# Two-block transformer on one core: the first scale taken as rows turned to columns, the first shift on VectorE, eight projection groups between them

## What is computed

```python
cond = jax.nn.silu(c)
mod = cond @ w_ada + b_ada                         # 2048 -> 6 * 2048
sh1, sc1, gt1, sh2, sc2, gt2 = jnp.split(mod, 6)
h = rms_norm(x, g_pre_mix) * (1.0 + sc1) + sh1
p = h @ w_in + b_in                                # 2048 -> 6 * 512 + 3 * 2048
u, v, q, k, v_att, z_pool, gates = jnp.split(p, ...)
y_sgu  = spatial_gating(gelu(u), gelu(v), ...)
y_moba = causal attention of 8 heads over q, k, v_att
y_pool = multiscale_pool(z_pool, ...)
merged = sigmoid(g_sgu) * (y_sgu @ w1) + sigmoid(g_moba) * (y_moba @ w2) + sigmoid(g_pool) * (y_pool @ w3)
x = x + gt1 * rms_norm(merged @ w_out, g_post_mix)
...                                                # a gated MLP, then a second block with attention, a state-space branch and an MLP
```

## Time and profile before

| | |
|---|---|
| median of 3 runs | 3094.23 us (3093.87 to 3096.17) |
| the profiled execution | 3090.89 us, its span 3089.1 us |
| busy: PE, DVE, ACT, POOL | 2988.6, 1816.6, 1262.7, 322.8 us |
| chain that ended last | PE 92%, DVE 3%, DMA 2% |
| bytes read from HBM | 647.26 MB |

### The profile page before, as it was taken

The page is one execution under the profiler, slowest core; times in us unless marked ns, Lnnn a source line. Parts: engine busy times, 40 slices in busy tenths (PEclk is TensorE's granted clock), DMA queues, the critical chain, the costliest instruction groups (busy, mean ns, idle before and its releaser), DMA issues.

```text
span 3089.1 us, 43195 instructions
## 1 busy us (share of the span) xinstructions
PE 2988.6 (97%) x18072; PEld 2591.9 (84%) x18072; DVE 1816.6 (59%) x1777; ACT 1262.7 (41%) x1208; POOL 322.8 (10%) x465
## 2 busy tenths in 40 slices
PE   8899999997999999999799999988999999999998
PEld 3488777886999999888688888877889999999886
DVE  1377777787667776544546447655555555555444
ACT  0133455435544444344534343334444344443343
POOL 1000000000000000000102956720000000000000
PEclk9899999998999999999899999999999999999999
DMA  9777777895666654555546652225655555555554
GB/s 363 275 270 269 282 280 285 302 351 210 232 226 236 233 215 179 206 207 215 194 147 222 219 198 75 91 75 204 234 188 182 197 193 190 192 193 210 207 210 170
DMA packets 109854, 666.51 MB, mean 216 GB/s; under 512 B 23472, under 2 KB 25680, under 8 KB 33296
## 3 DMA queue, kind: packets, MB, share of 16 engines
q1 hardware_dynamic: 101584, 626.96, 56.2%
q0 software_dynamic: 8144, 37.74, 3.3%
HBM read 647.26 MB, written 17.39 MB: 215 GB/s over the span
## 4 chain that ended last, share of the span: by engine, by line
PE 92%; DVE 3%; DMA 2%; ACT 1%; issue 1%; POOL 0%; SPq 0%; DVEq 0%; ACTq 0%; POOLq 0%
PE acc L2004 28%; PE acc L2006 27%; PE acc L2005 27%; PE ms L2078 3%; PE tp L2053 1%; DVE w_lo L1258 1%; DMA ada<-ada_stream 1%; DMA w_raw<-w_stream 1%; PE ms L2480 1%; PE acc L2509 0%; PE acc L2519 0%; DMA w_raw<-ada_stream 0%; PE ms L2479 0%; ACT w_hi L783 0%; ACT bias_rows L914 0%
## 5 line engine op out<-in xcount | busy, mean ns | idle before, releaser
L1258 DVE TENSOR_TENSOR w_lo<-w_raw,w_hi 128x2048 fp32r<-128x2048 f32 x484 | 1110.8, 2304 | 720.5 <-ACT w_hi L783 701.1
L783 ACT ACTIVATE w_hi<-w_raw 128x2048 fp32r<-128x2048 f32 x484 | 923.0, 1915 | 981.6 <-DMA w_raw<-w_stream 979.4
L2004 PE MATMUL acc<-h2T_hi,w_lo 128*128 128x256 f32 x2816 | 784.3, 279 | 0.0
L2005 PE MATMUL acc<-h2T_lo,w_hi 128*128 128x256 f32 x2816 | 783.3, 278 | 0.0
L2006 PE MATMUL acc<-h2T_hi,w_hi 128*128 128x256 f32 x2816 | 783.2, 278 | 0.0
L2005 PEld LDWEIGHTS acc<-h2T_lo,w_hi 128*128 128x128 f32 x2816 | 532.2, 189 | 0.0
L2006 PEld LDWEIGHTS acc<-h2T_hi,w_hi 128*128 128x128 f32 x2816 | 531.4, 189 | 0.0
L2004 PEld LDWEIGHTS acc<-h2T_hi,w_lo 128*128 128x128 f32 x2816 | 529.7, 188 | 0.0
L2004 PE MATMUL acc<-w_hi,hid_lo 128*128 128x512 f32 x704 | 275.6, 391 | 6.1 <-DVE w_lo L1258 6.1
L2005 PE MATMUL acc<-w_lo,hid_hi 128*128 128x512 f32 x704 | 275.0, 391 | 0.0
L2006 PE MATMUL acc<-w_hi,hid_hi 128*128 128x512 f32 x704 | 274.9, 390 | 0.0
(11 more groups left out here) (517 smaller groups left out, 3957.7 us busy)
## 6 DMA issues: line engine op xcount, KB each, us to landing
w_raw<-w_stream SPq DMA_DIRECT2D x484, 1024.0 KB, 4.8
ada<-ada_stream SPq DMA_DIRECT2D x64, 1024.0 KB, 6.9
w_raw<-ada_stream SPq DMA_DIRECT2D x32, 1024.0 KB, 4.9
g_dram<-gates_out SPq DMA_DIRECT2D x12, 512.0 KB, 7.1
gates_in<-g_dram POOLq DMA_DIRECT2D x12, 512.0 KB, 6.0
bias_rows<-b_in POOLq DMA_DIRECT2D x18, 256.0 KB, 6.0
x_res<-x POOLq DMA_DIRECT2D x2, 2048.0 KB, 13.7
g_dram<-gate_stage SPq DMA_DIRECT2D x8, 512.0 KB, 6.1
```

The costliest lines, as they stand in the source:

```text
L783: sc.activation(whi[:, s % 4], raw[:, s % 4], ACT.Copy).then_inc(hi_made, 1)
L1258: v.tensor_tensor(wlo[:, s % 4], raw[:, s % 4], whi[:, s % 4].bitcast(F32), ALU.subtract).then_inc(lo_made, 1)
L2004: mm(o, sl, mh, start=start, stop=False, skip_group_check=share)
L2005: mm(o, sh, ml, start=False, stop=False, skip_group_check=share)
```

## The change

Of the 32 groups of the front, PE keeps only the 16 of the scale. They use four new slots `ada_first` instead of `w_raw`. The 16 groups of the shift go the way of the later modulations, `ada_group` on DVE with the slots `ada1` (`first_shifts`). `x` is first scaled by its own `rstd` on DVE and turned to `xT` (32 transposes, copied by ACT alone). Each quarter `c` of the scale, a row, is copied by ACT (`row_copy`), turned to columns by four transposes, and the shift comes as columns from `mod_sum` by four matmuls with ones (`first_product`). `first_rows` on DVE and an Identity activation on ACT then make a quarter of `h1T_lo` and `h1T_hi` from `xT` with scale and bias of each partition. The bias rows become columns. `N_EARLY` = 8 projection groups, groups k = 0 to 3 of chunks 0 and 1 in turn, stand between the quarters; SP fetches their weights among the modulation groups. The 36 side groups stand ahead of the projection groups in `SIDE` (8, 10, 12, 13, 15, ... 70), and SP issues them two weight groups ahead of that. `ROUNDS1` and the calls between `to(s)` move accordingly.

```diff
+N_EARLY = 8
+SIDE = [N_EARLY + round(i * 62 / 35) for i in range(36)]
...
-            for j in range(4):
-                load(j, a["ada_stream"][j])
-            with sp.Fori(1, N_FRONT // 4) as i:
-                for j in range(4):
-                    sp.wait_ge(ada_used, (i - 1) * 4 + j + 1)
-                    load(j, row(a["ada_stream"], i * 4 + j))
-            for j in range(4):
-                sp.wait_ge(ada_used, N_FRONT - 3 + j)
-                load(j, a["w_stream"][j])
...
+            def first(p):
+
+                n, h = divmod(p, 2)
+                src = a["ada_stream"][h * 4 * GK + n]
+                if h:
+                    if n >= 2:
+                        sp.wait_ge(mod_used, n - 1)
+                    load_ada(ada1, n % 2, src)
+                else:
+                    if n >= 4:
+                        sp.wait_ge(ada_used, n - 3)
+                    sp.dma_start(adaf[n % 4][:].rearrange("p k c -> p (k c)"), src).then_inc(first_in[n % 4], 16)
+
+            def early(s):
+                if s >= 4:
+                    sp.wait_ge(pe_used, s - 3)
+                load(s % 4, a["w_stream"][s % 2 * 4 + s // 2])
+
+            for p in range(N_FRONT):
+                first(p)
+                if p >= 7 and p % 4 == 3:
+                    early(p // 4 - 1)
+            early(N_EARLY - 1)
...
-            for s in range(G_IN1):
+            for s in range(4, G_IN1):
                 sp.wait_ge(pe_used, s + 1)
                 load(s % 4, a["w_stream"][s + 4])
-                r = s // 2 - 1
-                if s % 2 == 0 and s and r + 2 < A_IN:
-                    sp.wait_ge(mod_used, r + 1)
-                    load_ada(ada1, r % 2, a["ada_stream"][N_FRONT + r + 2])
+                for r in range(A_IN - 2):
+                    if max(SIDE[r] - 2, 4) == s:
+                        sp.wait_ge(mod_used, A_FIRST + r + 1)
+                        load_ada(ada1, r % 2, a["ada_stream"][N_FRONT + r + 2])
...
-            turns_hi(h1T[0], KD)
+            act.wait_ge(ada_used, GK)
+            sc.activation(rowc[:], ms[0][:], ACT.Copy).then_inc(sem("row_copied"), 1)
+            for r in range(KD // 2):
+                act.wait_ge(tp_full, r + 1)
+                sc.activation(xflat[:, r * C:(r + 1) * C], tp[r % 2][:], ACT.Copy).then_inc(tp_free[r % 2], 1)
+            for c in range(4):
+                if c == 3:
+                    split()
+                    split()
+                if c > 0:
+                    act.wait_ge(ada_used, GK * (c + 1))
+                    sc.activation(rowc[:], ms[c % 2][:], ACT.Copy).then_inc(sem("row_copied"), 1)
+                act.wait_ge(sem("mod_evac"), c + 1)
+                for k in range(GK * c, GK * c + GK):
+                    ins = sc.activation(h1T[0][:, k], xT[:, k], ACT.Identity, scale=acol[:, k:k + 1], bias=scol1[:, k:k + 1])
+                ins.then_inc(sem("h1_hi"), 1)
+                if c < 3:
+                    split()
+                    split()
...
+            def first_rows(c):
+
+                dve.wait_ge(sem("shifts"), c + 1)
+                k = slice(GK * c, GK * c + GK)
+                b = ms[c % 2][:].rearrange("p (f s) -> p f s", s=P)
+                v.tensor_tensor(scol1[:, k], b[:, :, 1], bcol[:, 1, k], ALU.add)
+                chain(v.tensor_tensor(acol[:, k], b[:, :, 0], bcol[:, 0, k], ALU.add))
+                chain(v.scalar_tensor_tensor(acol[:, k], acol[:, k], 1.0, pcol[:, k], ALU.add, ALU.mult))
+                dve.sem_inc(sem("mod_evac"), 1)
...
+                for i in range(GK):
+                    kk = GK * c + i
+                    ins = v.tensor_scalar(xm[:, i], xT[:, kk], acol[:, kk:kk + 1], scol1[:, kk:kk + 1], ALU.mult, ALU.add)
+                chain(ins)
+                dve.wait_ge(sem("h1_hi"), c + 1)
+                v.tensor_tensor(h1T[1][:, k], xm[:], h1T[0][:, k].bitcast(F32), ALU.subtract).then_inc(sem("h1"), 1)
...
+            first_shifts(0, GK - 1)
+            rstd_wait()
+            for t in range(TT):
+                v.tensor_scalar(x[:, t], x[:, t], rstd[:, t:t + 1], None, ALU.mult).then_inc(sem("xn"), 1)
+            first_shifts(GK - 1, GK)
+            dve.wait_ge(sem("ld_first_cols"), 32)
+            for c in range(4):
+                if c < 3:
+                    first_shifts(GK * (c + 1), GK * (c + 1) + 2)
+                    first_rows(c)
+                    split()
+                    first_shifts(GK * (c + 1) + 2, GK * (c + 2))
+                    split()
+                else:
+                    split()
+                    split()
+                    first_rows(c)
...
-                    r = m.n // 2 - 1
-                    if m.n % 2 == 0 and r < A_IN:
+                    if m.n in SIDE:
+                        r = SIDE.index(m.n)
                         ada_group(ada1, macc1[r // 4 % 2], r % 4)
...
+            def first_product(c):
+
+                pe.wait_ge(sem("row_copied"), c + 1)
+                for f in range(4):
+                    tr(ms[c % 2][:, f * P:(f + 1) * P], rowc[:, f * P:(f + 1) * P], ident[:])
+                pe.wait_ge(mod_acc, c + 1)
+                for f in range(4):
+                    ins = mm(ms[c % 2][:, f * P + 1:f * P + 2], macc1[c % 2][:, f * P:(f + 1) * P], ones[:], start=True, stop=True)
+                ins.then_inc(sem("shifts"), 1)
...
+            for c in range(2):
+                early(2 * c)
+                first_mods(c + 1, 2, GK)
+                first_mods(c + 2, 0, 1)
+                first_product(c + 1)
+                early(2 * c + 1)
+                first_mods(c + 2, 1, 2)
+            early(4)
+            first_mods(3, 2, GK)
+            first_product(3)
+            early(5)
+            early(6)
+            early(7)
```

More of the change, by code:

```diff
@@ L197, in block_program @@
         gb1 = [u(f"gates_in{j}", [P, TT, C], 32 + 4 * j) for j in range(3)]
-        h1 = u("h1", [P, TT, D], 56)
+        adaf = [u(f"ada_first{j}", [P, GK, C], 40 + 8 * j) for j in range(4)]
+        xT = u("xT", [P, KD, S], 72)
+        xm = u("x_mod", [P, GK, S], 100)
+        rowc = u("row_copy", [P, C], 88.5)
         tril = u("tril", [P, P], 88)
-        row1, rowT1 = u("row1", [P, 2, D], 32), u("rowT1", [P, D], 48)
         y3T = [u("y3T_hi", [P, 3, 4, S], 64, F32R), u("y3T_lo", [P, 3, 4, S], 76, F32R)]
@@ L297, in block_program @@
         ada_in = [sem("ada_in0"), sem("ada_in1")]
+        first_in = [sem(f"first_in{i}") for i in range(4)]
         mod_used, mod_acc, mod_sum = sem("mod_used"), sem("mod_acc"), sem("mod_sum")
@@ L2101, in rows_group, with early @@
                 end_group(ins)
+            first_mods(0, 0, GK)
+            pe.wait_ge(sem("ones"), 1)
+            pe.wait_ge(sem("ld_ident"), 16)
+            pe.wait_ge(sem("xn"), TT)
+            for k in range(KD // 2):
+                turn([(x[:, t, (2 * k + q) * P:(2 * k + q + 1) * P], q * S + t * P) for q in range(2) for t in range(TT)])
+            first_product(0)
+            first_mods(1, 0, 2)
+            chunks.add(2)
+            def early(n):
+                if n % 2 == 0:
+                    pe.wait_ge(sem("h1"), n // 2 + 1)
+                rows_group(bank(n % 2), h1T, n // 2)
+            for c in range(2):
[11 more added lines that the diff above has]
+            early(7)
+            sums = Tally()
+            sums.add(GK)
             def to(s):
@@ L2170, in _ @@
             to(15)
-            product(1)
-            to(16)
+            product(0)
+            to(18)
             pe.wait_ge(sem("y_sgu"), 1)
@@ L2235, in _ @@
                     pv1(hp - 1, 3)
+                if hp == 1:
+                    product(3)
                 if hp == 3:
@@ L2240, in _ @@
                 to(b + 3)
+                if hp == 0:
+                    product(2)
                 if hp == 2:
+                    pe.wait_ge(sem("mod_cols"), 1)
+                    ring("mod_rows1")
+                    turn([(mcol[:, 0:D // P], 0)])
                     product(5)
@@ L2256, in _ @@
             pv1(3, 3)
-            to(68)
-            pe.wait_ge(sem("mod_cols"), 1)
-            ring("mod_rows1")
-            turn([(mcol[:, 0:2 * D // P], 0)])
+            to(69)
+            product(8)
             to(71)
-            product(8)
             def merged_turns(n):
```

185 lines of the change are left out of this document (82 added, 103 removed).

## The result

The changed kernel takes 3053.52 us (median of 4 runs, 3052.61 to 3054.43) where the kernel before takes 3095.20 on the same chip (3093.87 to 3101.02). The ratio is 0.9863, with a 95% interval of 0.9851 to 0.9875: 41.7 us less, against 47.5 forecast. 3047 was named, 3038 to 3064 was the range.

The account below looks back on a forecast made before the run. PE was taken to bound the front and the first projection. Group 7 ending 49.0 us sooner, less 1.5 for tight places, gave 47.5 us less: 3043.4 for the profiled execution, median 3047, range 3038 to 3064.

Parts of the forecast that it names:

- Start of group 0: Front: shift group 5 lands at 40.6 us, and the series behind it lets PE start group 0 at 51.
- PE's sum to the end of group 7: Front from group 0 on: PE is never out of work, 86.0 us added up, group 7 ends at 137.0.
- The cold start: At group 0 after PE's idling: 14 matmuls at 0.43 us in place of 0.23, 2.9 us.
- Rival A: Front: transfers are the bound at 327 GB/s, group 7 ends at 148, gain 36.5 us, 3058; chance 0.10.
- Rival E: Front: quicker than the sum, no cold start and group 0 at 48, gain 53.5 us, 3041; chance 0.07.
- Groups 8 to 71: First projection behind group 7: 395.53 us before, same PE work after, 1.5 us more for tight places.
- three places are tight: evac(0) ahead of group 8, mod_cols(0) behind 15, product 5 behind 47: 0 to 1 us each, 1.5 in all.
- The sign named for this stage: Groups 8 to 71: about 395 to 398 us from the product behind group 7 to the stage's last product.
- Rival B: Groups 8 to 71: DVE late at 18 odd groups, PE waits about 1 us each, gain 31, 3063; chance 0.12.
- Rivals C and D: Front clock. C: low throughout, 3125 us, chance 0.03. D: only scale groups 1 to 5 cold, 3050, in likeliest case.
- Rival F: Behind the front: no change, since later waits give the gain back; chance 0.02.
- everything behind it is the same work: Behind the end of group 7: same work in both kernels, so no difference was forecast behind group 71.

Follow-up runs that it names:

- e7: Changed kernel plus ten unread float32 matmuls of 512 columns on PE ahead of group 0: 3047.60 us, ratio 0.9842.
- e5: Changed kernel with the first quarter of h1T_lo and first w_lo on DVE ahead of shift groups 4 to 7: 3052.61 us, ratio 0.9863.
- e6: Changed kernel with the edits of e1 and e5 together: 3038.59 us, ratio 0.9824.
- e11: e6 with mod_cols(0) behind w_lo 17 and product 7 behind group 62: 3037.88 us, ratio 0.9822.
- e1: Changed kernel with ACT's copy of mod_rows1 behind w_hi of group 49 instead of ahead of it: 3048.33 us, ratio 0.9843.
- e10: e1 with side groups ahead of even groups 8 to 70 and 15, 29, 43, 57, sooner fetch kept: 3038.71 us, ratio 0.9827.
- e8: e1 with side groups fetched behind the weight group they stand ahead of, not two groups sooner: 3080.20 us, ratio 0.9948.
- e4: Changed kernel plus eight unread float32 matmuls of 512 columns on PE ahead of group 0: 3048.35 us, ratio 0.9853.
- e2: Changed kernel with the eight early projection groups behind the whole front instead of between its quarters: 3070.93 us, ratio 0.9921.

## Why the prediction was right, and where not

- **Start of group 0: right, 1.6 us short** (51 forecast, 52.6 measured). The series behind the landing of shift group 5 was forecast as 10.1 us and took 10.1 (42.48 to 52.60), the Identity steps at 2.07 where 1.7 was taken, within the bounds. The landing came at 42.4 instead of 40.6. The transfers averaged 395 GB/s up to it, and the sum's own average is 400 (16.25 MB in 40.6 us), which is 0.5 us. The other 1.3 are bytes: 16.75 MB had moved by then, 0.5 more than the sum has ahead of this group.
- **PE's sum to the end of group 7: right.** 86.0 us forecast, 85.9 measured (52.60 to 138.50, where the matmul behind group 7 starts). The terms hold one by one: three scale groups in 10.3 us (60.91 to 71.21) as forecast, a `first_product` 1.25 where 1.47 was taken, the row copy 0.69 where 0.8 was. The cold start forecast as 2.9 is what e7 took away. Rival A is out: behind group 0, PE waits 0.69 us in all, and the transfers kept 405 to 426 GB/s from 20 to 100 us. Rival E named 48 for group 0; e5, e6 and e11 had 43 to 45 and came 0.6, 2.4 and 1.2 us sooner at group 7, not much more than the 1.1 us over which group 7 varies with one and the same front, because the waits move to the transfers.
- **Groups 8 to 71: the step that was mis-sized**, "three places are tight ... each could cost PE 0 to 1; I take 1.5 in all". It was 6.8. Of that 6.0 is one wait with the slow matmuls behind it (e1; 4.8 in five other executions). The other 0.8 is `product` 8, which the sentence "the same matmuls, turns and products after" had overlooked: it came into this stage from behind it. Product 5 behind group 47 was named, but as DVE's lateness. What it was is ACT's wait for the turn that now stands in the same place, `mod_rows1`, which the change had moved there from behind group 68, and I had not asked what is queued behind the copy: `w_hi` of the next group, in an engine that is busy for 182 of 402 us. The sign named for this stage, 395 to 398 us, failed in the changed kernel and holds with e1's edit. Of the other two places, `evac(0)` cost nothing and `mod_cols(0)` 0.6 us. Product 7 behind 61 was not named and cost 0.3 (group 62 takes 7.44 us in e1, and 7.15 in e10, where its sums are ready).
- **Rival B: out in its form.** In e1 all 18 odd places are in use and the stage takes 396.3 us. But the mechanism is real once the fetch is late: e8, 34.7 us. The prediction gave SP's slack as a group, and the sooner fetch only as "can take away the 29.6 us that DVE waits for `ada`". In fact the stage depends on it. The waits themselves fell as far as was named: the 120 rows had 33.0 us of idling ahead of them, and the 132 in e1 3.9.
- **Rivals C and D.** The granted clock was 0.92, 0.91 and 0.74 in the windows of 4 to 24, 20 to 40 and 40 to 60 us, and 1.00 from 60 on. Neither cost anything beyond the forecast cold start, but D's fall of the clock did come once: PE waited 2.98 us for scale group 2, the granted clock of 21 to 25 us was 0.58, and groups 2 and 3 took 8.65 us where 7.03 is the pace at the upper level. PE had 8.82 us in hand ahead of group 0, so the 1.6 us were not on its path. That agrees with the rule of the Trainium skill (TensorE: Matmul & The Clock Gate, section HAM oscillation), though not at every wait: 1.86 us of waiting for group 1 brought no fall (1.00 from 14 to 20 us). It bears on e5 too, where a wait of 3.83 us was followed by a slow burst and one of 1.86 by a group partly at the lower clock.
- **Rival F: out.** The interval of the ratio ends at 0.9875.
- **Behind group 71: "everything behind it is the same work" was right of the work but for `product` 8, and not of the time.** It took 4.2 us more. Up to `w_lo` 75 it was 2.6 us less. From `w_lo` 75 to 285 the changed kernel took 1237.3 us and the one before 1232.7, the other versions 1234.8 to 1242.1, all with the same code: 4.6 more, with PE idle for 46.3 us against 43.7, the difference ahead of matmuls that wait for `w_lo`. From 285 to 315, where the clock fell in both profiled executions, it was 337.0 against 334.3: 2.6 more. What sets these I did not find, and it stays open.

The sum of the three rows of the table, -36.5 us, is the difference of the spans but for rounding. The medians differ by 41.7: that of before lies 4.3 above its profiled execution (3090.89), that of the changed kernel 0.9 below its own (3054.43). That part is luck. The forecast for the profiled execution was 3043.4, and it missed that by 11.0 us; it missed the median by 6.5.

## What to carry to other kernels

When a turn or product moves behind another group, list for every engine that waits for it what stands behind that wait in its own queue. The engine with half its time idle was the one that cost 6 us. When loads are spread more evenly, the smallest distance between issue and use counts, not the mean: 5.4 us where a load takes 7.4 cost 34.7 us, although DVE had a quarter of its time free. Once a front is at PE's sum, starting it 8 to 9 us sooner gave 0.6 to 2.4 us, and keeping PE busy up to its start gave 1.9 to 3.1.

## What the runs showed of the hardware

- The clock fell after short waits, and not always: 1.94 us of idling in e4 (three matmuls at full rate, then 0.43 us steps), 1.86 in e5, but 1.80 at the same place in e6 without a fall, and 1.66 us with a fall in the changed kernel and none in e6. At that last place the stretch is some 8 us longer where the clock fell (mean 335.3 against 327.5). The Trainium skill (TensorE: Matmul & The Clock Gate, section Part 1: The HAM clock gate) calls the change run-variable, because the observation runs free of the kernel's start; two outcomes of one wait agree with it.
- Four `x_mod` steps of 128x256 on DVE took 1.38 us in the changed kernel and 3.33 at one place in e2. There the first of them, begun 0.13 us behind a POOL TENSOR_TENSOR of 2.34 us, took 2.36 us and ended 0.15 behind it; the other three took 0.40 each, as in the changed kernel (0.41).
